# A four-part transformer in one kernel: expert products joined, start and MLA stage re-cut, 30 early blocks instead of 26

## The reference

```python
q = (t @ w_q).reshape(n_tok, PEER_HEADS, 2, SUB_DIM)
sc = jnp.einsum("thpd,hpnd->thpn", q, subkeys)
sv, si = lax.top_k(sc, PEER_TOPK)
...
top_v, pos = lax.top_k(cand, PEER_TOPK)
idx = jnp.take_along_axis(cidx, pos, axis=-1)
g = jax.nn.softmax(top_v, axis=-1)
...
u = jnp.take(u_tab, ic, axis=0)
h = jnp.einsum("cd,ced->ce", xc, u)
a = gc * jax.nn.gelu(h, approximate=False)
return jnp.einsum("ce,ced->cd", a, jnp.take(v_tab, ic, axis=0))
```

## Time and profile before

| | |
|---|---|
| median of 3 runs | 2785.22 us (2783.14 to 2787.93) |
| the profiled execution's own time | 2784.15 us |
| its span, first to last instruction | 2782.3 us |
| mean granted TensorE clock | 0.971 |
| busy, PE / PEld / DVE | 2582.9 / 2317.0 / 1797.5 us |
| busy, ACT / POOL | 1299.3 / 784.6 us |
| HBM read | 418 MB, 151 GB/s over the span |

### The profile page before, as it was taken

One profiled execution on the slowest core, in us unless ns is written; L12 is line 12 of the kernel. 1 busy time (PEld: TensorE's weight loads), 2 busy tenths in 40 slices (PEclk: granted clock), 3 DMA queues, 4 the chain that ended last, 5 costly groups with the idle time before them and its releaser, 6 DMA issues.

```text
span 2782.3 us, 47349 instructions
## 1 busy us (share of the span) xinstructions
PE 2582.9 (93%) x15959; PEld 2317.0 (83%) x15959; DVE 1797.5 (65%) x3387; ACT 1299.3 (47%) x1919; POOL 784.6 (28%) x786
## 2 busy tenths in 40 slices
PE   7879987899899888999999999889888999999998
PEld 5679865798789787899999998669787899999997
DVE  5768755687557998455555555567997555555555
ACT  4656545565444165444444444454165444444443
POOL 0300003000000101355555555230101355555554
PEclk9999999999999999999999999989999999999999
DMA  5135641356554413666666665424413666666664
GB/s 187 53 122 182 191 125 46 114 182 189 159 167 136 136 39 106 185 187 187 183 188 187 183 188 180 121 76 132 126 39 121 184 188 186 184 187 186 184 188 143
DMA packets 170078, 420.43 MB, mean 151 GB/s; under 512 B 13968, under 2 KB 66637, under 8 KB 169726
## 3 DMA queue, kind: packets, MB, share of 16 engines
q1 hardware_dynamic: 162894, 412.82, 48.4%
q10 hardware_dynamic: 7088, 6.33, 0.8%
HBM read 418.02 MB, written 1.08 MB: 151 GB/s over the span
## 4 chain that ended last, share of the span: by engine, by line
PE 77%; DVE 15%; ACT 3%; issue 3%; DVEq 1%; POOL 1%; SPq 0%; ACTq 0%; DMA 0%; POOLq 0%
PE PS L447 24%; PE PS L449 24%; PE PS L448 24%; DVE oh L1887 3%; DVE oh L1884 1%; DVE lo L1337 1%; DVE arena L1850 1%; PE PS L602 1%; DVE arena L1854 1%; DVEq L1887 1%; DVE arena L1784 1%; DVE arena L1788 1%; DVE arena L1785 1%; ACT arena L976 1%; DVE arena L1472 0%
## 5 line engine op out<-in xcount | busy, mean ns | idle before, releaser
L1337 DVE TENSOR_TENSOR lo<-raw,hi 128x1024 fp32r<-128x1024 f32 x732 | 1007.6, 1381 | 777.3 <-ACT hi L908 775.1
L908 ACT ACTIVATE hi<-raw 128x1024 fp32r<-128x1024 f32 x732 | 765.8, 1055 | 502.1 <-PE PS L449 483.9
L447 PE MATMUL PS<-xh,hi 128*128 128x256 f32 x2784 | 791.7, 284 | 2.6 <-DVE xl L1385 2.6
L448 PE MATMUL PS<-xl,hi 128*128 128x256 f32 x2784 | 791.5, 284 | 0.0
L449 PE MATMUL PS<-xh,lo 128*128 128x256 f32 x2784 | 791.3, 284 | 0.0
L447 PEld LDWEIGHTS PS<-xh,hi 128*128 128x128 f32 x2784 | 536.4, 193 | 12.9 <-issue 4.1
L448 PEld LDWEIGHTS PS<-xl,hi 128*128 128x128 f32 x2784 | 536.6, 193 | 8.0
L449 PEld LDWEIGHTS PS<-xh,lo 128*128 128x128 f32 x2784 | 536.3, 193 | 0.0
L447 PE MATMUL PS<-hi,Ah 128*128 128x512 f32 x1024 | 403.9, 394 | 10.8 <-DVE lo L1337 7.1
L449 PE MATMUL PS<-hi,Al 128*128 128x512 f32 x1024 | 404.7, 395 | 0.0
L448 PE MATMUL PS<-lo,Ah 128*128 128x512 f32 x1024 | 404.1, 395 | 0.0
(11 more groups left out here) (224 smaller groups left out, 2968.3 us busy)
## 6 DMA issues: line engine op xcount, KB each, us to landing
raw<-in_peer_u SPq DMA_DIRECT2D x256, 512.0 KB, 3.6
raw<-in_peer_v SPq DMA_DIRECT2D x256, 512.0 KB, 4.3
raw<-in_ffn_w_up SPq DMA_DIRECT2D x88, 512.0 KB, 3.6
raw<-in_ffn_w_down SPq DMA_DIRECT2D x44, 512.0 KB, 3.8
raw<-in_peer_w_q SPq DMA_DIRECT2D x32, 512.0 KB, 4.7
raw<-in_da_w_qkv SPq DMA_DIRECT2D x24, 512.0 KB, 4.0
raw<-in_conv_w_in SPq DMA_DIRECT2D x24, 512.0 KB, 3.6
raw<-in_attn_w_qkv SPq DMA_DIRECT2D x12, 512.0 KB, 4.2
```

The lines of the kernel that those rows point to most:

```text
L447: pe.matmul(o, ah, bh, start=start, stop=False)
L448: pe.matmul(o, ah, bl, start=False, stop=False)
L908: cp.activation(hi[:, s, 0:size], raw[:, s, 0:size], ACT.Copy).then_inc(hi_made, 1)
L1337: V.tensor_tensor(lo[:, s, 0:size], raw[:, s, 0:size], hi[:, s, 0:size].bitcast(F32), ALU.subtract).then_inc(lo_made, 1)
```

## The change

1. **The product of x and u in the main loop is joined.** `xh` and `xl` become the halves of one tensor `xx`; for each slice one matmul of 512 columns (hi by xh and xl at once) and one of 256 (lo by xh) take the place of three of 256. The two halves of the bank have to be added: a new DVE instruction, `add_parts` (line 1977), reduces 512 PSUM columns to 256 in `gl`, and ACT's gelu now reads and writes `gl`. PE waits for h_summed where it waited for gelu_made.
2. **The start.** The host lays all parameters out as columns or rows; SP loads x in halves, the identity and the columns and goes on to the weights, ACT issues 7 more loads; PE's turning of parameters goes away, the table of the GQA bias moves behind two groups of `da_qkv`, and a first Sqrt stands ahead of ACT's squares.
3. **MLA.** The q part is squared, scaled and turned when group 0 of `mla_in` is there; the kv part follows, and is turned behind group 0 of `mla_uq`. The rope of q stands behind groups 0 and 1 of `mla_ukv`.
4. **LEAD 26 to 30**, LEAD_FIRST 18 to 20, and 10 early blocks between the batches. The four further rows lie in X[:, 0]; half of x (512 KB) goes to DRAM behind u block 0 and comes back behind v block 28.

```diff
-LEAD = 26
-LEAD_FIRST = 18
-LEAD_AFTER = (3, 11, 19, 27, 35, 43, 51, 63)
+LEAD = 30
+LEAD_FIRST = 20
+LEAD_AFTER = (3, 9, 15, 21, 27, 33, 39, 45, 51, 63)
 KEPT = LEAD - 2
+IN_X = D // T
...
-            if j < KEPT:
+            if j < KEPT - IN_X:
                 return kept[:, j - 16, :]
+            if j < KEPT:
+                return X[:, 0, (j - KEPT + IN_X) * T:(j - KEPT + IN_X + 1) * T]
...
                     if i >= LEAD + 2:
-                        pe.wait_ge(gelu_made, h0 + i - 1 + exa)
+                        pe.wait_ge(h_summed, h0 + i - 1 + exa)
...
-                        m = mm3(PS[:, 6 + i % 2, 0:T], hi[:, s, w], lo[:, s, w], xh[:, k, :], xl[:, k, :],
-                                k == 0, k == KD - 1)
+                        both = PS[:, 6 + i % 2, :].rearrange("p (c t) -> p c t", c=2)
+                        pe.matmul(both, hi[:, s, w], xx[:, :, k, :], start=k == 0, stop=False)
+                        m = pe.matmul(both[:, 0, :], lo[:, s, w], xh[:, k, :], start=False, stop=k == KD - 1)
...
-            pe.wait_ge(params_in, 16 * N_PARAMS)
-            pe.wait_ge(S("params_more"), 32)
-            pe.wait_ge(S("rows_in"), 6 * 16)
...
+            pe.wait_ge(S("mla_c_made"), 2)
+            turn("mcq", lambda t, k: proj[:, t, k * P:(k + 1) * P])
+            pe.wait_ge(xt_lo, xt["mcq"][0] + 3)
+            rows_linear("mla_uq", [([2, 1], 512, 0)] * 3, {0: turn_kv})
...
-                    act.wait_ge(split_used, u_block(layer, i) + 1 + 2 * exa)
-                    act.wait_ge(S("a_made"), a0 + i - 1 + exa)
-                    cp.activation(gl[:, i % 2, :], PS[:, 6 + i % 2, 0:T], ACT.Gelu).then_inc(S("gelu_made"), 1)
+                    act.wait_ge(S("h_summed"), (P - LEAD) * layer + i - LEAD + 1 + exa)
+                    cp.activation(gl[:, i % 2, :], gl[:, i % 2, :], ACT.Gelu).then_inc(S("gelu_made"), 1)
...
-                with dve.Fori(0, left // 4, 1) as it:
-                    for p in range(p0, p0 + 4):
-                        split(M + p, BLK, it * 4)
...
+                def add_parts(i, ex=0):
+
+                    dve.wait_ge(split_used, u_block(layer, i) + 1 + 2 * ex)
+                    dve.wait_ge(S("a_made"), P * layer + i - 1 + ex)
+                    V.tensor_reduce(gl[:, i % 2, :], PS[:, 6 + i % 2, :].rearrange("p (c t) -> p t c", c=2), AX.X,
+                                    ALU.add).then_inc(S("h_summed"), 1)
...
+                with dve.Fori(0, (P - LEAD - 2) // 2, 1) as it:
+                    for x in range(2):
+                        add_parts(LEAD + x, it * 2)
+                        split(M + p0 + 2 * x, BLK, it * 4)
+                        split(M + p0 + 2 * x + 1, BLK, it * 4)
...
                 for i in range(LEAD):
                     u_in(i)
+                    if i == 0:
+                        sp.wait_ge(xs_made, 4 * norms["n7" if layer else "n5"][2] + 4)
+                        sp.dma_start(aside, X[:, 0, :]).then_inc(S("x_aside"), 16)
...
                 v_in(LEAD - 2)
+                sp.wait_ge(S("lead_weighed"), LEAD * layer + KEPT)
+                sp.wait_ge(S("x_aside"), 16 * (layer + 1))
+                sp.dma_start(X[:, 0, :], aside).then_inc(S("x_back"), 16)
```

More of the change, by code:

```diff
@@ L819, in _ @@
                 rows_group(B + 4 * g, G0 + g, [2] * 4, 512)
+            pe.wait_ge(params_in, 16 * N_PARAMS)
+            b = aux("rel", [(S("rel_table"), 1)])
+            pe.matmul(PS[0:GQA_H, b, :], relv[0:BUCKETS + 1, :], hotv[0:BUCKETS + 1, :],
+                      start=True, stop=True).then_inc(aux_full, 1)
             with pe.Fori(0, 2, 1) as it:
@@ L916, in splits_to, with turned @@
                     nxt[0] += 1
-            def turned(name, gain):
+            def turned(name, gain, first=0):
                 base, kcs = xt[name]
```

241 lines of the change are left out of this document (132 added, 109 removed).

## The result

The changed kernel takes **2736.14 us** (median of 4 runs, 2735.6 to 2737.39) against 2784.62 us for the kernel before (2783.14 to 2787.93 on the same chip): a ratio of 0.9825, 95% interval 0.9808 to 0.9842. It is 48 us faster. The forecast was 2786 us; the time lies in the range, on the spot of the first rival, "POOL gets in (clean rounds)", 2737 us. The profiled execution spans 2733.9 us, against 2782.3 us before.

A forecast was written before the change was run, and what follows sets the result against it. PE was taken to bound the main loop and DVE the one-hot stage. 2784.15 - 23.0 + 1.4 - 11.8 + 50 + 1.4 - 8.5 - 7 = 2786.7, say 2786 us; range 2729 to 2800.

The forecast's parts named there:

- POOL gets in (clean rounds): Main loop: POOL is served between the two queued DVE splits, no round waits, 2737 us; chance 0.27.
- The step that failed: Main loop: DVE goes straight from u split to v split, POOL waits, every second round pays 0.51 us, +50 us.
- the likeliest case: Main loop: every second round pays a PE wait for POOL, 2786 us, own range 2774 to 2799; chance 0.58.
- The slow one: Rival, main loop: the wait of about 0.5 us comes back in each of 196 rounds, 2835 us; chance 0.08.
- Early blocks: Expert layers: four more early blocks each take 8 u blocks of 2.87 us out of the PE-bound loop, -23.0 us.
- the joined product: Main loop: each slice costs 7.5 ns less, 8 slices x 196 blocks, -11.8 us; bounds nothing and 20 us.
- the loop's end: Last round of each main loop: POOL, already late, is later with the reduction; 0.7 us a layer, +1.4 us.
- Two blocks ahead of the turning: Before the choice is turned: two early blocks make the first transposes 3.7 us late, costing 0.7, +1.4 for both layers.
- Reduction: Main loop on DVE: reducing 512 PSUM columns takes 0.68 us, with 0.4 and 1.2 as ends.
- x put aside: Expert layers: two 512 KB DMAs per layer on SP cost nothing; if the cover fails, up to 3 us a layer.
- Start: Kernel start: first product near 14.5 us, 9.3 earlier, bias table costs 0.8; -8.5 us, ends -4 and -11.
- MLA: MLA stage: gaps give 6.5, rope 1.7 won, kv part costs about 1; -7 us, ends -2 and -11.

The follow-up runs named there:

- the dose: Changed kernel with a copy of 128 (small) or 512 (large) PSUM columns ahead of each reduction on DVE; 2759.82 us and 2839.39 us.
- the experiment: Changed kernel with only the main loop's joined product undone (three products per slice, gelu straight from PSUM, no DVE reduction); 2749.15 us, ratio to before 0.9869.

## Why the prediction was wrong, point by point

- **The step that failed** is in the term for the reduction: "the v split is ready 0.17 us before the u split ends, DVE goes straight on, and by the earlier trace rows POOL waits for it too". Its premise was right (ready 0.18 us ahead), its conclusion was not, in any round: Al ended at +4.94, 1.08 us ahead of the end of the v split, and PE had no wait. With it fell the +50 us. 2786.7 less 50 is 2737 us, 1 us from the measured time. That it is so close is in part luck: the start gave 5.2 us less than its term, and the GQA stage, which no term has, 4.3 us more in the profiled execution, by its clock. How early the v split is ready does not matter (0.9 us ahead with the dose).
- **What I read wrongly** was the weight of one row. The earlier trace rows is one place that occurs once a layer; I made it a rule for 196 rounds. The trace of before held the very case once inside the loop, in its last round, which I had not looked at. DVE's timeline, then POOL's, of the kernel before:

```profile
1731.81 3.27 DVE L1337 TENSOR_TENSOR lo<-raw,hi 128x1024 fp32r<-128x1024 f32 x2 [3.85 <-ACT hi L908]
```

```profile
1732.41 1.59 POOL L2019 TENSOR_TENSOR Al<-kept,Ah 128x256 fp32r<-128x256 f32 x1
```

  Two splits without idle time between them, 3.27 us where two undisturbed ones take 2.35 (at 17.61 in the changed kernel's trace), and an Al of 1.59 us that asked during the first: POOL was let in between them. These lines contradict the likeliest case, at the same instructions. They would have turned the chances around.
- **The rivals.** The clean case was right, for a better reason than I gave. The slow one had its threshold too high: I let it decide from a reduction of 0.95 us, by POOL's chain alone. By the doses DVE's own circle sets the round from 0.06 to 0.09 us beyond the 0.69 measured, that is from 0.75 to 0.78 us. I had summed the way to PE and not the way back to the next reduction.
- **Early blocks** -23.0: right. With the joined product -11.8 and the loop's end +1.4 the forecast for loops and early values was -33.4; measured -32.8. The rounds of a joined and an unjoined loop differ by the forecast 0.060 us. The Trainium skill ("TensorE: Matmul & The Clock Gate", back-to-back issue gap) puts the cost beyond the columns at some 2.5 ns a matmul, which would give 3.9 us, an estimate; the experiment gave 13.0 in the median and 10.2 in the loops, end included. The measurement decides.
- **Two blocks ahead of the turning** +1.4: measured -0.3. PE's transposes did start 3.2 us later in the stage (forecast 3.7), but the copy behind them came only 0.13 us later, since DVE was busy with its own chain until 959.37 anyway, as it had been before:

```profile
958.95 0.42 DVE L1911 TENSOR_TENSOR arena<-arena,small 128x256 f32<-128x256 f32 x1
959.40 1.02 DVE L1918 COPY selT<-PS 128x512 f32<-128x512 f32 x2
```

- **Reduction** 0.68: 0.69. **x put aside** 0: right, shown by taking it away.
- **Start** -8.5: the first matmul came 8.68 us earlier, but only 3.3 us of that were left at the end of the product. Behind the earlier start the splits met DVE's lambda chain and memsets, which the term had not followed; the forecast's lower end, -4, was crossed. The step missing was "what on DVE stood in the cover of the late start". It is 5.2 us off its term, over the 5 us that the forecast had named as a sign of being wrong.
- **MLA** -7: -7.15 in the stage. The first two gaps gave 5.4 us where I had 6.5. The rotary gave 4.6 us ahead of the attention and cost 2.5 in mla_ukv, 2.1 net where I had 1.7 (4.6 less some 3). By subtraction 0.4 us went elsewhere in the stage, where I had put 1 for the kv part.
- **GQA**: its -4.3 us was in no term, and is not the change's (see the section on the hardware).

## What to carry over

When a forecast hangs on who wins between two engines, look for the case in the trace at the same instructions, the last and first rounds of the loop included, before taking a rule from another place; one instance with another history is no rule. When a start is pulled forward, list what else stands on each engine in the time that was its cover, since it becomes the next wait. And close the circle: a chain through several engines that just meets PE may already bind on its way back to itself.

## What the runs showed of the hardware

- DVE and POOL hold each other off for whole instructions, and in the loops the waiting POOL is let in between two queued DVE instructions: in every round with queued instructions, with one to three of them ready behind the boundary. Among the early values it is passed over at three boundaries in a row, 36 times of 38, and at one in the other two. What sets these apart was not found. The Trainium skill ("GPSIMD Engine Reference", specifications) says that the two contend for the SBUF interface; the traces agree, with 1.81 us for a split held by POOL and 1.23 for one that isn't.
- The same program's stages outside the expert layers vary with the granted clock. The GQA stage took 201.90 us at 0.91 in the profile of before, and in the kernel before with one added DVE instruction, whose GQA stage is the same code, 197.70 us at 0.94:

```profile
1741.70:1943.60 201.90, 174.40 (x1043) 154.37 (x1042) 130.03 (x378) 101.64 (x182) 41.48 (x36) 0.91 0.37 110
```

```profile
1742.00:1939.70 197.70, 166.16 (x1030) 146.87 (x1029) 128.46 (x357) 102.58 (x189) 40.01 (x36) 0.94 0.37 115
```

  The changed kernel gave 197.57 in one profile and 201.80 in another. So a difference of 4 us in that stage is no effect of an edit, while the loops and one-hot stages repeat within 0.05 us.
